# A hybrid encoder trunk on one core: x is turned into six PSUM banks, its split parts are read straight from them, and the row sums are taken before the turn

## The reference, cut to what matters

```python
def rmsnorm(x, w):
    y = x * rsqrt(mean(x * x, axis=-1) + EPS)
    return y * w

# even layer
h = rmsnorm(x, norm_w)
proj = h @ w_in                       # 1024 -> 9 sections of 1024
qa, ka, va, ga, qh, ffw, fbw, ih, gh = split_cols(proj, EVEN_SIZES)
lam = exp(sum(lp[0] * lp[1])) - exp(sum(lp[2] * lp[3])) + lam_init
oa = differential_attention(rope(qa), rope(ka), va, lam) * silu(ga)
ob = hgrn2_bidirectional(qh, ffw, fbw, ih) * silu(gh)
x = x + concat(oa, ob) @ w_out
# odd layer: windowed attention with 32 heads, gate, output projection
# then: x = rmsnorm(x, final_norm)
```

## Time and profile before

| | |
|---|---|
| median of 3 runs | 1158.93 us (1157.7 to 1159.53) |
| profiled execution, its own time | 1158.41 us |
| its span, first to last instruction | 1156.6 us |
| TensorE matmul busy | 1127.6 us, 97% |
| VectorE busy | 977.4 us, 85% |
| ScalarE busy | 677.1 us, 59% |
| DMA | 103.60 MB, mean 90 GB/s |

### The profile page before, as it was taken

How to read it: one execution, slowest core, us unless ns; L and a number is a source line. 1 busy time by engine, 2 the same in 40 slices (tenths; PEclk the granted TensorE clock), 3 DMA queues, 4 the chain that set the end, 5 groups by cost and what they waited for, 6 DMA issues and landing times. The chain is left out here.

```text
span 1156.6 us, 18631 instructions
## 1 busy us (share of the span) xinstructions
PE 1127.6 (97%) x5750; PEld 913.4 (79%) x5750; DVE 977.4 (85%) x1927; ACT 677.1 (59%) x1324; POOL 0.2 (0%) x4
## 2 busy tenths in 40 slices
PE   6999999999999999999999999999999999999996
PEld 5877778778778778778778877887888888888875
DVE  6879889889889889789789898888888888888886
ACT  6474564564564564564654674366666666666654
POOL 0000000000000000000000000000000000000000
PEclk9999999999999999999999999999999999999999
DMA  7613422522422423323324220554232324323112
GB/s 211 158 56 92 138 64 56 145 65 58 130 73 61 121 73 75 107 73 86 96 73 98 85 73 19 124 137 122 80 91 54 91 66 120 101 59 91 55 38 73
DMA packets 131817, 103.60 MB, mean 90 GB/s; under 512 B 5440, under 2 KB 116416, under 8 KB 131776
## 3 DMA queue, kind: packets, MB, share of 16 engines
q1 hardware_dynamic: 131776, 103.07, 32.7%
HBM read 77.88 MB, written 2.10 MB: 69 GB/s over the span
## 5 line engine op out<-in xcount | busy, mean ns | idle before, releaser
L74 PE MATMUL bank_proj<-hH,w_hi 128*128 128x512 f32 x856 | 343.1, 401 | 1.3 <-issue 1.2
L76 PE MATMUL bank_proj<-hH,w_lo 128*128 128x512 f32 x856 | 334.5, 391 | 0.0
L75 PE MATMUL bank_proj<-hL,w_hi 128*128 128x512 f32 x856 | 334.3, 391 | 0.0
L76 PEld LDWEIGHTS bank_proj<-hH,w_lo 128*128 128x128 f32 x856 | 160.8, 188 | 35.2
L74 PEld LDWEIGHTS bank_proj<-hH,w_hi 128*128 128x128 f32 x856 | 161.5, 189 | 32.8 <-issue 1.9
L75 PEld LDWEIGHTS bank_proj<-hL,w_hi 128*128 128x128 f32 x856 | 161.4, 189 | 30.9 <-issue 0.5
L1943 ACT ACTIVATE probs<-bank_odd_score,small 128x256 f32<-128x256 f32 (+1 forms) x128 | 66.3, 525 | 73.9 <-DVE small L2181 73.9
L1220 DVE TENSOR_TENSOR w_lo<-w_raw,w_hi 128x1024 fp32r<-128x1024 f32 x74 | 89.4, 1217 | 9.3 <-ACT w_hi L710 9.3
L710 ACT ACTIVATE w_hi<-w_raw 128x1024 fp32r<-128x1024 f32 x74 | 78.0, 1055 | 28.9 <-DMA w_raw<-in_w_in_even 28.4
L1950 ACT ACTIVATE probsT<-bank_odd_turn 128x256 fp32r<-128x256 f32 (+1 forms) x128 | 49.0, 434 | 61.8 <-PE bank_odd_turn L1677 61.7
L775 ACT ACTIVATE probs<-bank_score,small 128x512 f32<-128x512 f32 x64 | 43.4, 684 | 60.0 <-DVE small L1058 53.2
(11 more groups left out here) (412 smaller groups left out, 2219.0 us busy)
## 6 DMA issues: line engine op xcount, KB each, us to landing
w_raw<-in_w_in_even SPq DMA_DIRECT2D x72, 512.0 KB, 4.9
w_raw<-in_w_in_odd SPq DMA_DIRECT2D x36, 512.0 KB, 4.4
qs<-parts SPq DMA_DIRECT2D x96, 128.0 KB, 2.3
ks<-parts SPq DMA_DIRECT2D x40, 256.0 KB, 4.4
o_raw<-in_w_out_even SPq DMA_DIRECT2D x15, 512.0 KB, 6.2
o_raw<-in_w_out_odd SPq DMA_DIRECT2D x14, 512.0 KB, 6.7
out<-w_raw SPq DMA_DIRECT2D x8, 256.0 KB, 2.1
mixT<-in_x SPq DMA_DIRECT2D x2, 512.0 KB, 5.4
```

The source lines that it names most:

```text
L74: pe.matmul(out, hi, moving_hi, start=start, stop=False)
L75: pe.matmul(out, hi, moving_lo, start=False, stop=False)
L76: return pe.matmul(out, lo, moving_hi, start=False, stop=stop)
```

## The change

x is turned into the banks S0, S1, T, O, W and PB2, and for the last two tiles S0 and S1 again, so the transposes of the first six tiles wait for no copy. `hH` and `hL` are made straight from the banks. Of the copies to `xT` ScalarE keeps the first and VectorE does the other seven, of which six stand behind the low parts of the weights of projection -1. The right half of x is loaded behind the first weights. The squares are taken on x as it was loaded, with a row on a partition: four ScalarE instructions that also sum each row of 1,024 elements; VectorE spreads the four columns of sums, and TensorE turns them (four transposes) in place of the product with ones, now behind 6 steps of projection -1. On TensorE the transposes of the values stand behind 5 steps of projection 1. On VectorE lambda's first steps and the rope's scaling stand ahead of `low` for projection 1, and `low` for projection 2 ahead of the second rotation.

```diff
+        XB = [S[0], S[1], T, O, W, PB[2], S[0], S[1]]
+        KEPT = (1, 2, 5, 3, 4, 6, 7)
 # sync
+            load_x(0)
             load(0, -2)
+            load_x(1)
             load(0, -1)
 # TensorE
-                if k >= 2:
-                    pe.wait_ge(x_kept[k % 2].sem, x_kept[k % 2].at(0, k // 2))
+                if k == 6:
+                    pe.wait_ge(raw.low.sem, raw.low.at(0, 1))
+                if k >= 6:
+                    pe.wait_ge(x_kept[k % 2].sem, x_kept[k % 2].at(0, 1))
                 for t in range(NC):
-                    mm = pe.transpose(S[k % 2][:, t * P:(t + 1) * P], x_tiles[t // 2][:, t % 2, k * P:(k + 1) * P],
+                    mm = pe.transpose(XB[k][:, t * P:(t + 1) * P], x_tiles[t // 2][:, t % 2, k * P:(k + 1) * P],
                                       eye[:])
...
             proj(0, -2)
-            proj(0, -1, 0, 5)
-            rms.sum(pe, T)
-            proj(0, -1, 5)
+            proj(0, -1, 0, 6)
+            pe.wait_ge(rms.added.sem, rms.added.at(0, 1))
+            pe.wait_ge(x_kept[1].sem, x_kept[1].at(0, 2))
+            for t in range(NC):
+                mm = pe.transpose(T[:, t * P:(t + 1) * P], x_rstd[:, t * P:(t + 1) * P], eye[:])
+            mm.then_inc(rms.summed.sem, 1)
+            proj(0, -1, 6)
+            pe.wait_ge(x_kept[1].sem, x_kept[1].at(0, 3))
             proj(0, 0)
-            proj(0, 1, 0, 2)
+            proj(0, 1, 0, 5)
             pe.wait_ge(PB[2].free.sem, PB[2].free.at(0, 0))
             turn(0, 1, vt)
-            proj(0, 1, 2)
+            proj(0, 1, 5)
 # ScalarE
-            keep_x(0)
             high_x(0)
+            high(0, -2)
             high_x(1)
...
+            keep_first_x()
+            for k in range(2, KT):
+                high_x(k)
             high(0, -1)
-            for k in range(KT):
-                rms.square(act, k)
+            for t, into in enumerate((decay, soft, turned, probs)):
+                for i in range(2):
+                    act.wait_ge(x_landed[i].sem, x_landed[i].at(0, 2 if i else 3))
+                act.activation(into[:, :, :].rearrange("p a t -> p (a t)"), x_tiles[t // 2][:, t % 2, :], ACT.Square,
+                               accum_out=x_squares[:, t:t + 1]).then_inc(rms.squared.sem, 1)
             high(0, 0)
+            rms.root(act, T)
             high(0, 1)
-            rms.root(act, T)
 # VectorE
+            low_x = lambda k: raw.split_low(dve, k, XB[k][:])
+            low_x(0)
             low(0, -2)
+            low_x(1)
+            keep_x(KEPT[0])
+            for k in range(2, KT):
+                low_x(k)
             low(0, -1)
-            for k in range(1, KT):
-                rms.add(dve, k)
+            for k in KEPT[1:6]:
+                keep_x(k)
+            dve.wait_ge(rms.squared.sem, rms.squared.at(0, NC))
+            dve.tensor_copy(chunked(x_rstd[:]), x_squares.unsqueeze(2).broadcast_to([P, NC, P])).then_inc(rms.added.sem, 1)
+            keep_x(KEPT[6])
             low(0, 0)
-            low(0, 1)
             first_lambda()
             scale_rope()
+            low(0, 1)
             rotate(-1, 7)
             scale_vt(0, 0, 0)
+            low(0, 2)
             rotate(-1, 8)
-            low(0, 2)
             last_lambda()
```

More of the change, by code:

```diff
@@ L125, in __init__, with split_high, split_low @@
         self.xT, self.w, self.hH, self.hL = xT, w, hH, hL
-    def split_high(self, act, k):
-        act.activation(self.hH[:, k], self.xT[:, k], ACT.Copy, scale=self.w[:, k:k + 1]).then_inc(self.high.sem, 1)
-    def split_low(self, dve, k):
+    def split_high(self, act, k, of=None):
+        of = self.xT[:, k] if of is None else of
+        act.activation(self.hH[:, k], of, ACT.Copy, scale=self.w[:, k:k + 1]).then_inc(self.high.sem, 1)
+    def split_low(self, dve, k, of=None):
+        of = self.xT[:, k] if of is None else of
         dve.wait_ge(self.high.sem, self.high.at(0, k + 1))
-        dve.scalar_tensor_tensor(out=self.hL[:, k], in0=self.xT[:, k], scalar=self.w[:, k:k + 1],
+        dve.scalar_tensor_tensor(out=self.hL[:, k], in0=of, scalar=self.w[:, k:k + 1],
                                  in1=self.hH[:, k].bitcast(F32), op0=ALU.mult,
@@ L208, in even_layer @@
         total = small[:, 40:48].rearrange("p (d c) -> p d c", d=2)
+        x_squares = small[:, 48:48 + NC]
         att = attT[:, 0:NC * SEQ].rearrange("p (s t) -> p s t", s=NC)
@@ L321, in _, with load_x @@
             sp.dma_start(wn[:, 0], norm).then_inc(norm_landed.sem, DMA)
-            for i in range(2):
+            def load_x(i):
                 for a in range(2):
@@ L694, in _, with keep_first_x, high_x @@
             act.preload_act_table_set(EXP_LOG)
-            def keep_x(k):
+            def keep_first_x():
+                act.wait_ge(x_turned.sem, x_turned.at(0, 1))
+                act.wait_ge(raw.low.sem, raw.low.at(0, 1))
+                act.activation(xT[:, 0], XB[0][:], ACT.Copy).then_inc(x_kept[0].sem, 1)
+            def high_x(k):
                 act.wait_ge(x_turned.sem, x_turned.at(0, k + 1))
[L697 to L701, removed]
+                raw.split_high(act, k, XB[k][:])
             def high(h, n):
@@ L995, in keep_x @@
                 dve.wait_ge(x_turned.sem, x_turned.at(0, k + 1))
-                dve.tensor_copy(xT[:, k], S[1][:]).then_inc(x_kept[1].sem, 1)
+                dve.tensor_copy(xT[:, k], XB[k][:]).then_inc(x_kept[1].sem, 1)
             def scale(h, n, into):
```

10 lines of the change are left out of this document (removed).

## The result

The changed kernel took 1159.65 us (median of 20 runs, 1157.39 to 1161.55) against 1158.01 us for the kernel before in the same number of runs (1156.42 to 1159.53). The ratio is 1.0015, interval 1.0009 to 1.0021: slower by 1.0 to 2.4 us. The ratio itself is under the 0.2% that the prediction called no change, the interval's upper end reaches it. 1160.0 us had been forecast. The profiled execution took 1161.37 us, 1.7 above the median, with a span of 1159.2 us.

What follows compares the result with a forecast made beforehand. TensorE, busy for 97% of the span, was taken as the bound, with the key move setting the scores' start. 1158.41 + 0.1 (later scores) + 1.6 (lower clock) = 1160.1 us, forecast as 1160.0; range 1156.9 to 1161.8.

Steps and rivals of the forecast that it cites:

- Which wait decides: Ahead of the first scores: the key move sets their start, leaving TensorE idle for about 2.4 us.
- The fall of the clock: Behind the idle time ahead of the scores: TensorE at half speed for 3.41 us, costing 1.6 us.
- Rival (a): At the scores: the wait comes but the clock does not fall, 1158.5 us; chance 0.24.
- Step 1: Load order: x's second half lands at 12.2 us, first weights near 9.2 us, ending the weights' wait at 16.02 us.
- Step 2: Transposes of x in six banks: about 1.2 us idle, projection starts at 15.0 to 15.7 us, effectively 15.6.
- Rival (b): Amid the transposes: idle time delays the clock's rise, 1.4 us lost in the projection, 1161.6 us; chance 0.14.
- Step 3: Row sums: TensorE does not wait; the root is ready 11.6 us behind the projection's effective start, 0.6 us earlier.
- Step 4: VectorE's order: the key chain from the root takes 12.2 us against 10.9, moved splits costing 1.3 to 1.5 us more.
- The sum: Whole kernel: scores start at 46.4 us against 46.27, 0.1 us lost, plus 1.6 us for the clock.

Runs made afterwards that it cites:

- sums_early: The changed kernel with only the row sums turned behind 2 steps of projection -1 instead of 6; 1156.69 us, ratio 0.9989 to the kernel before.
- keys_first: The changed kernel with row sums behind 2 steps of projection -1, first rotation ahead of low weights 1, values' transposes behind 7 steps of projection 1; 1155.53 us.
- order_alone: The kernel before with only VectorE's new order of scaling, low weights and second rotation; 1158.83 us, ratio 1.0011 to the kernel before.
- rotation_back: The changed kernel with the low weights of projection 2 behind the second rotation on VectorE again; 1157.8 us, ratio 0.9996 to the kernel before.
- filled: The changed kernel with 11 more matmuls of unused result between projection 2 and the first scores; 1157.1 us, ratio 0.9994 to the kernel before.
- loads_back: The changed kernel with x loaded whole ahead of the first weights, their split behind the parts of tile 3; 1158.8 us, ratio 1.0008 to the kernel before.
- keys_first_warm: `keys_first` with 24 matmuls of ones, result unused, on TensorE before x has landed; 1154.79 us, ratio 0.9976 to the kernel before.

## Why the prediction was right

- **Which wait decides.** Right, and shown. The new wait is where it was forecast (2.68 us, forecast 2.4) and its cause is the key chain: a chain that starts 2.7 us earlier shrinks it to 1.5 us (`sums_early`), a chain short enough takes it away (`keys_first`), and VectorE's new order makes it alone (`order_alone`). `rotation_back` adds nothing here, since its chain kept its length.
- **The fall of the clock.** Right, and shown: with the idle time filled, the scores' own chain is as long and the loss is gone, and with it parted in two (`rotation_back`) most of the loss is gone as well. Rival (a), the wait without the fall, did not come. At this place the clock fell behind 2.68 and 2.61 us and held behind 1.5 to 1.9 us. The gap's length alone does not decide: behind the idle 2.4 us near 105 us it fell in 6 of the 12 profiles, and behind the 1.59 us near 1134 us, ahead of which stand gaps of 0.7 and 0.2 us, in 8 of 12. The price of 1.6 us is met by the profiled execution, but 6.2 us at the lower clock in `loads_back` cost about 3. What decides between one price and the other was not tested.
- **Step 1.** The second half of x landed at 3.78 + 8.3 = 12.1 us (forecast 12.2). The idle time amid the transposes was 0.81 us, not 1.2.
- **Step 2 was mis-sized on its fast side.** I read 0.68 us a tile at the higher clock from the earlier trace rows, but these tiles waited for copies; a tile takes 0.43 us. So the start lies between 13.7 us (`filled` and `keys_first_warm`) and 15.5 with about 1.3 us more at the lower clock, an effective 16.1, and not between 15.0 and 15.7. The executions differ by this: part of the wider scatter of the changed kernel. In the profiled one the slow side came, 0.5 us worse than the 15.6 taken.
- **Rival (b) came in part.** It said that the idle time amid the transposes delays the clock's rise, to 18.5 us, and lets that decide from 17.5 us on. In the profiled execution the pace doubled near 16.8 us, against 13.6 us before. Of the six profiles with this idle time (0.8 to 0.95 us) all tiles behind it ran at 0.86 us in four, and at 0.43 us in two; of the six profiles without it none had its last two tiles at the slow pace. So the delay is likely real but doesn't come each time. `loads_back`, which takes the idle time out, is 0.8 us faster than the changed kernel by the ratios, with overlapping intervals.
- **Step 3.** The root ended at 27.70 us, 11.6 us behind the effective start of 16.1, as worked out. The four squares with their sums took 17.41 to 21.66 us, 4.3 and not 5, and TensorE did not wait.
- **Step 4.** 12.2 us from root to keys, as worked out. The key moves took 7.3 us to the scores instead of 7.0. Together with the start that makes 47.20 us where 46.4 was forecast.
- **The sum.** Forecast +1.7 us on the profiled execution and 1160.0; measured +1.6 between the medians. The agreement is partly luck. In the profiled execution the scores' wait and fall cost 2.5 us and not 1.7, since the start cost more; a third fall near the end came on top, and 1.4 us that nobody forecast came back over the loops of heads. The 20 runs lie in three groups, near 1157.6 (3 runs), 1159.5 (10) and 1161.3 (7). Steps of 1.7 us would fit the number of falls, of which the profiled run, in the top group, has two besides the one that before had. But the start alone differs by up to 2.4 us between executions, and the mean granted clocks of the middle and the top group are alike (0.993 to 0.995 and 0.993 to 0.994). So what makes the groups is not shown.

## What to carry to other kernels

Moving a start earlier gives nothing if a chain on another engine, here root, rotations and key moves, already ends at the next wait: measure from the common event to each wait's end, and count every instruction that a reordering puts into that chain. Idle time of TensorE can cost more than itself, since matmuls behind it may run at the lower clock. Here filling it with matmuls of no use gave back about 2.5 us and parting it about 2, though a chain short enough to remove it gave most, about 4. An instruction taken out of a chain gains no more than the slack to the next wait in it: in `rotation_back` 1.2 us of work left the chain, and a wait for an older DMA took 1.0 of them. Two lists written by hand have to be changed together: a weight's high half behind the root on one engine needs its low half behind the root's user on the other.

## What the runs showed of the hardware that was not expected

Transposes alone bring the higher clock. In `loads_back` TensorE did nothing but transposes from 7.55 us on; the four tiles up to 11.02 us took 0.86 us each, the next three 0.43 to 0.48. When the clock rises differs between executions of kernels that are alike up to there: behind the idle 0.8 us amid the transposes the tiles took 0.86 us in the changed kernel's profile and 0.43 in that of `filled`. Nor did 24 small matmuls of ones from 1.50 to 6.88 us change the pace of the tiles right behind them: about 0.86 us each from 7.36 us on.

The length of an idle gap alone did not tell whether the clock fell: the same 2.4 us were followed by a fall in half of the profiles. A fall lasted 3.4 us where it came, but once, behind the idle 2.61 us in `loads_back`, about twice that.
